# Prompt attention: a unit's last key block is transposed ahead of its first one, and each of the two waits for the query tiles that it reads alone

## The reference

```python
k = mla_keys(c_kv, k_r, w_uk, ...)                     # (T, 8 heads, 96)
v = jnp.einsum('btr,rhv->bthv', c_kv, w_uv)            # (T, 8 heads, 128)
s = jnp.einsum('bqhd,bkhd->bhqk', qi, k) * SCALE
s = jnp.where(k_pos[None, :] <= q_pos[:, None], s, -jnp.inf)
p = jax.nn.softmax(s, axis=-1)
o = jnp.einsum('bhqk,bkhv->bqhv', p, v)
```

## Time and profile before

| | us |
|---|---|
| median of 3 runs | 2067.64 (2067.43 to 2069.14) |
| the profiled execution, and its span | 2069.43, 2067.6 |
| PE busy | 2027.0 (98% of the span) |
| DVE busy | 1273.2 (62%) |
| ACT busy | 857.2 (41%) |
| POOL busy | 551.9 (27%) |
| mean granted TensorE clock | 0.997 of full |

### The profile page before, as it was taken

The page is one execution under the profiler, slowest core; times in us unless marked ns, Lnnn a source line. Parts: engine busy times, 40 slices in busy tenths (PEclk is TensorE's granted clock), DMA queues, the critical chain, the costliest instruction groups (busy, mean ns, idle before and its releaser), DMA issues.

```text
span 2067.6 us, 35685 instructions
## 1 busy us (share of the span) xinstructions
PE 2027.0 (98%) x12489; PEld 1866.4 (90%) x12489; DVE 1273.2 (62%) x2492; ACT 857.2 (41%) x1691; POOL 551.9 (27%) x562
## 2 busy tenths in 40 slices
PE   7999999999999999999999999989999999999999
PEld 6889999988889999999999978879988899998888
DVE  5674411277777777767767753576666656666665
ACT  5552111166656656666665642422222222222221
POOL 2210000044431334534553520022232222223220
PEclk9999999999999999999999999999999999999999
DMA  5243222335322222222222161101211111121112
GB/s 173 83 107 80 63 85 84 100 98 153 108 72 78 73 72 68 63 67 69 67 62 71 55 237 43 42 21 47 76 41 41 41 41 41 43 79 41 41 41 87
DMA packets 146270, 152.41 MB, mean 74 GB/s; under 512 B 50710, under 2 KB 122118, under 8 KB 145101
## 3 DMA queue, kind: packets, MB, share of 16 engines
q1 hardware_dynamic: 140405, 128.02, 20.6%
q0 software_dynamic: 5728, 22.65, 3.4%
HBM read 124.77 MB, written 25.97 MB: 73 GB/s over the span
## 4 chain that ended last, share of the span: by engine, by line
PE 88%; DVE 5%; ACT 3%; issue 2%; DMA 1%; SPq 0%; POOL 0%; ACTq 0%; DVEq 0%
PE ps L105 16%; PE ps L2324 16%; PE ps L107 16%; PE ps L106 16%; PE ps L859 12%; PE ps L1755 2%; PE ps L819 2%; PE ps L1472 1%; PE ps L1714 1%; PE ps L1720 1%; PE ps L2413 1%; DVE pa_ntop L1319 1%; PE ps L776 1%; PE ps L869 1%; ACT pa_prob L1234 1%
## 5 line engine op out<-in xcount | busy, mean ns | idle before, releaser
L2576 DVE TENSOR_TENSOR t_m<-t_m,ps 128x512 f32<-128x512 f32 x256 | 172.1, 685 | 112.6 <-PE ps L107 112.6
L1828 ACT ACTIVATE sq<-ps 128x512 f32<-128x512 f32 x256 | 153.3, 599 | 204.0 <-PE ps L107 202.8
L105 PE MATMUL ps<-f_late_h 128*128 128x512 f32 x512 | 200.2, 391 | 7.4 <-issue 6.9
L106 PE MATMUL ps<-f_late_l,f_late_h 128*128 128x512 f32 x512 | 200.0, 391 | 0.0
L107 PE MATMUL ps<-f_late_h,f_late_l 128*128 128x512 f32 x512 | 199.8, 390 | 0.0
L1915 DVE TENSOR_REDUCE ss<-sq 128x8 f32<-128x512 f32 x256 | 173.0, 676 | 0.0
L2429 POOL TENSOR_TENSOR f_bl<-f_x,f_bh 128x512 fp32r<-128x512 f32 x45 | 59.6, 1325 | 364.5 <-ACT f_bh L2419 364.5
L1913 DVE TENSOR_TENSOR g_attn_b<-ps,g_attn_b 128x64 f32<-128x64 f32 x256 | 56.8, 222 | 147.1 <-ACT sq L1828 145.5
L105 PEld LDWEIGHTS ps<-f_late_h 128*128 128x128 f32 x512 | 96.5, 188 | 27.8 <-issue 8.1
L2519 ACT ACTIVATE f_late_h<-f_raw 128x2048 fp32r<-128x2048 f32 x15 | 28.8, 1919 | 219.9 <-PE ps L107 219.9
L107 PEld LDWEIGHTS ps<-f_late_h,f_late_l 128*128 128x128 f32 x512 | 96.5, 189 | 20.2
(11 more groups left out here) (473 smaller groups left out, 6313.1 us busy)
## 6 DMA issues: line engine op xcount, KB each, us to landing
f_raw<-in_w_ff SPq DMA_DIRECT2D x32, 1024.0 KB, 5.8
c_ring<-in_cache_kv_latent SPq DMA_DIRECT2D x192, 128.0 KB, 2.0
m_raw<-in_w_in SPq DMA_DIRECT2D x20, 512.0 KB, 4.0
gated<-gate POOLq DMA_DIRECT2D x8, 1088.0 KB, 4.8
pa_gm<-gated SPq DMA_DIRECT2D x16, 512.0 KB, 4.6
c_early<-in_cache_kv_latent SPq DMA_DIRECT2D x64, 128.0 KB, 2.0
fr_x<-in_x_prompt SPq DMA_DIRECT2D x8, 512.0 KB, 3.7
mixed<-pa_mixed SPq DMA_DIRECT2D x16, 256.0 KB, 2.1
```

What stands on the lines that cost most here:

```text
L105: nc.tensor.matmul(out, lh, rh, start=first, stop=False)
L106: nc.tensor.matmul(out, lh, rl, start=False, stop=False)
L1828: nc.scalar.activation(sq[:, j % 2, :].rearrange("p (a n) -> p a n", a=2), ps[:, kn_bank(j):kn_bank(j) + 2, 0:HALF], ACT.Square).then_inc( ...
L2576: nc.vector.tensor_tensor(out, out, ps[:, 4 + p % 4, :], ALU.add).then_inc(S["y"], 1)
```

## The change

`order_of` puts the last block ahead of block 0: 4, 0, 1, 3, 2 and 8, 0, 1, 7, 2, 6, 3, 5, 4. Everything else in the list of items stays, the banks too. The wait for the scaled row tiles now stands at both of the first two blocks, each for the tiles that it reads alone: the narrow block for the first scaled tile of the unit, block 0 for all four. Block 0 must still be the first product of the unit, so the narrow block's product is now issued behind it. In units with pieces between the blocks, block 0's product thereby moves from item 5 to item 6, behind that item's piece. The slot wait of a unit's fifth block counts one product more.

```diff
     def order_of(qc):
         rest = [kt for kt in range(NK) if P * kt - META < QC * (qc + 1)]
-        head = [rest.pop(0)]
+        head = [rest.pop(-1), rest.pop(0)]
         while rest:
-            head.append(rest.pop(-1))
+            head.append(rest.pop(0))
             if rest:
-                head.append(rest.pop(0))
+                head.append(rest.pop(-1))
         return head
...
+    first_blocks = [block_no[blocks_of[u][0]] for u in range(len(units))]
...
                     if block_no[n] >= 4:
-                        act.wait_ge(S["pv"], block_no[n] - 3)
+                        act.wait_ge(S["pv"], block_no[n] - 3 + (block_no[n] - 4 in first_blocks))
...
-                if j == blocks_of[u][0] and u:
+                if kt == 0 and u:
                     pe.wait_ge(S["out"], u)
...
-            firsts = [blocks_of[u][0] for u in range(len(units))]
+            firsts, seconds = ([blocks_of[u][k] for u in range(len(units))] for k in range(2))
...
                         if n == blocks_of[p][0]:
                             if p == 0:
                                 pe.wait_ge(S["padded"], SEQ // P - 1)
-                            pe.wait_ge(S["scaled"], NT * (p + 1))
+                        if n in blocks_of[p][0:2]:
+
+                            pe.wait_ge(S["scaled"], NT * (p + 1) - max(0, i - 1 - NT * qc))
...
-                if n - 4 in firsts:
-                    product(n - 4)
                 if n - 3 in block_no and n - 3 not in firsts:
                     product(n - 3)
+                if n - 3 in seconds:
+                    product(firsts[seconds.index(n - 3)])
```

## The result

| | before | after |
|---|---|---|
| median of 5 runs (us) | 2069.14 (2067.43 to 2071.79) | 2079.03 (2076.87 to 2079.93) |
| the profiled execution, span | 2069.43, 2067.6 | 2079.13, 2077.4 |
| PE busy | 2027.0 | 2030.1 |
| mean granted TensorE clock | 0.997 | 0.996 |

The change makes the kernel slower: 1.0046 times before [1.0035, 1.0057], 9.9 us by these medians. The median of before is that of the three runs known ahead (2067.64) and two more. The instruction counts of PE, DVE, ACT and POOL are the same. PE is busy 3.1 us longer with the same matmuls, a first sign that some of them ran at a lower clock; the rest of the difference is time in which PE stands idle.

The account below looks back on a forecast made before the run. PE was taken to bound the prompt's attention (busy 547.21 of 550.00 us). Losses of 0.3 + 1.1 + 2.85 + 0.65 + 2.6 = 7.5 us on 2069.43, less 1.79, gave 2075.1 us; 8-in-10 range 2067 to 2079.5.

Parts of the forecast that it names:

- the clock's case: Units 4 and 8: PE stands still 2.9 us and the clock falls, 3.4 us more, 2078.5; chance 0.10.
- Part 1: First block of units 3, 7, 11, 13: work moved ahead of the wait for POOL gains 1.5 us, at most 3.5.
- Part 2: Units 2, 6, 10: item 6's projection waits for the wide low half behind the gate; 1.0 us late.
- Part 3: Units 3, 7, 11: exponential ahead of the wide copy delays the gate; 0.95 us per pair with the unit before, 0.65 for 12, 13.
- Part 4: Units 4 and 8: low half 0.53 us later and the covering product now behind the projection; 1.3 us each, 2.6 together.
- Part 5: Units 1, 5, 9: PE's fifth item waits for the now wide low half behind the gate; 0.37 us net each, 1.1 together.
- Part 6: The rest: unit 0 loses 0.3 us; units 14 and 15 and the stricter slot wait cost nothing.
- the small gain: Rival: waits at POOL shrink and nothing else moves; 1.5 us won, 2066.1; chance 0.15.
- the faster one: Rival: gate follows the narrow low half at once in units 1, 5, 9, 4, 8; 4.15 us won, 2063.5; chance 0.07.
- The clock's rival: Units 4 and 8: the long stand-still of PE lowers the clock, 1.7 us each, 2078.5; chance 0.10.

Follow-up runs that it names:

- e6: The changed kernel with POOL subtracting only 16 of 1024 columns of q's low half for heads 2 to 7; 2071.51 us, 1.001 times before.
- e4: The changed kernel with DVE's low half put between the gate's multiplication and addition; 2069.07 us, 0.9999 times before.
- e8: The changed kernel with item 1's exponential behind item 2's copy in units 3, 7, 11, 13, DVE's reciprocal one item later; 2080.37 us, 1.0043 times before.
- e3: The changed kernel with eight unread matmuls more on PE ahead of item 6's projection in units 4 and 8; 2077.46 us, 1.0038 times before.
- e2: The change made in odd units alone, even units keeping the order of before; 2072.91 us, 1.0013 times before.
- e7: The kernel before with the stricter slot wait alone; 2069.81 us, 1.0002 times before.
- e9: The kernel before with DVE's low half between the gate's steps and, in even units 2 to 12, the addition four items later; 2066.4 us, 0.9982 times before.
- e10: The changed kernel with DVE's low half between the gate's steps and, in even units 2 to 12, the addition four items later; 2068.13 us, 0.9992 times before.
- e5: The kernel before with DVE's low half put between the gate's multiplication and addition; 2067.2 us, 0.9988 times before.
- e1: The change made in even units alone, odd units keeping the order of before; 2077.2 us, 1.0036 times before.

## Why the prediction was right, and where it was not

The direction was right and the size short: a sum of 7.5 us, against 9.4 by units and 9.9 by the medians. The forecast, 2075.1, is 3.9 us under the median: 2.4 of these are the size, 1.5 the base, since it started from 2067.64 and before's median with two more runs is 2069.14. The measured 2079.03 lies within the range by 0.5 us, and just above the forecast's own range (2071 to 2079): it is covered because the range was drawn out to the clock's case, which had a chance of 0.10.

- **Part 1** (four waits for POOL won in part): the waits went. But "L1475's wait for POOL is still there in units 3, 7, 11, about as long" was wrong, and by the prediction's own numbers: PE comes 1.0 late and does 0.37 more ahead of the wait, the scaling is about 0.6 late, so 0.82 becomes 0.05. The timeline of unit 3 shows none, and one of 0.5 is left in the prompt's attention. Since the times followed from the sum and not from that sentence, they held.
- **Part 2** (1.0 for each of units 2, 6, 10): measured 0.97, 0.96, 0.96, by the step foreseen; e6 shows the cause in POOL's subtraction and e4 in DVE's order. The wait itself is 0.67 where I wrote about 0.9: the view counts it from the transposes' end (458.05), whereas the product that stood there in the kernel before started 0.24 ahead of theirs (457.31 and 457.55).
- **Part 3** (0.95 for each pair, 0.65 for 12 and 13): 0.93, 0.92, 0.89 and 0.53. e8 shows the reversed order of copy and exponential, with 0.3 for each odd unit.
- **Part 4** (**1.3 us** each for units 4 and 8): 2.59 and 2.48. **This is the term that was mis-sized.** The low half and the product behind the projection cost 1.02 and 1.06 (e3), a little under 1.3: in e3's unit 4 the scores of item 7 are 1.17 later than in before, counted from the unit's first scores, and 0.16 come back behind them. The other 1.57 and 1.42 are the clock. I had it as a rival with a chance of 0.10, priced at 1.7 each, and argued from waits of 1.0 us at the same place that left the clock alone. They say nothing on one of 2.79: the prediction itself had worked out 2.9 us in one piece. The rule that it named, of the Trainium skill, TensorE: Matmul & The Clock Gate, section "Why this matters for your kernels", is that gaps between bursts of matmuls drop the clock, and the trace agrees: it fell in both units. The page says only roughly how long a gap must be, and 2.79 us stands at the edge of its wording, so it did not settle the case ahead of the run. In e6's profile 1.63 us in the same place did not lower the clock.
- **Part 5** (0.37 for each of units 1, 5, 9): 0.35, 0.33, 0.35. In e2, with even units as before, they pay the same: the order of the odd unit alone does it.
- **Part 6**: unit 0 lost nothing where 0.3 was forecast, units 14 and 15 nothing beyond the queries' stretch, the slot wait nothing (e7).

Parts 2 and 3 come to 3.3 us, part 4 to 5.1, part 5 to 1.0, u15 to 0.2. Waits were forecast at some 16 us, the view has 14.4. Of the rivals, the small gain did not come, and the faster one failed on both its conditions. The gate did not follow the narrow low half at once, and it was not POOL that stood between, as the prediction had it: in unit 4 DVE first waits 2.38 us for ACT's copy of the values (`pa_v`, 481.44), 2.37 before, and less the 1.4 that the units ahead hand over the multiplication starts when it did before (482.79 and 481.36). And PE did wait for the wide low half behind the gate. The clock's rival, 2078.5, is 0.5 us under the median, in part by luck: its sum of 10.9 is 1.0 too large and its base 1.5 too low.

What stays open: e4 leaves 0.16 to 0.48 in units 3, 7, 11 and 13, and wins 0.39 in units 1, 5 and 9; I have no experiment that takes these apart.

## What to carry to other kernels

When two blocks are swapped to shorten one wait, look where their follow-up work lands in the other engines' queues: here most of the loss came from a 0.69 us instruction that fell behind one that took 1.85 beside another engine's instruction, and putting the instruction that frees a bank ahead of the one that frees nothing brought the time back to that of before. Forecast not only the sum of PE's waits but how long it stands still in one piece: here the long pause cost the wait and then the slower matmuls behind it, and the second part was the larger one (1.57 and 1.42 us against 1.02 and 1.06). And try such a repair on the old kernel too: with the two moves on DVE the kernel before (e9) is ahead of the changed one (e10). To put the held instruction one place later only moved the wait (e5); to put it behind the subtractions left 0.3 us of it (e9).

## What the runs showed of the hardware that I had not expected

In ten of the twelve profiles the clock stands low for a while at the samples' queries (612.7 in the earlier trace rows), though PE is busy, and the length differs from profile to profile: none in e1 and e7, 3.4 us in after, some 6.8 in e2 and e3. e7, e2 and after:

```profile
606.00:616.00 10.00, 10.00 (x86) 9.26 (x85) 7.17 (x15) 4.98 (x13) 3.12 (x4) 1.00 0.25 79
```

```profile
613.80:620.60 6.80, 6.80 (x40) 6.45 (x39) 2.40 (x5) 1.12 (x3) 0.96 (x2) 0.50 0.15 58
```

```profile
622.70:626.10 3.40, 3.40 (x22) 3.17 (x21) 1.45 (x3) 0.43 (x3) 0.00 (x0) 0.50 0.00 0
```

Measured against before this is worth from -1.5 (e1) to +2.0 us (e9) in u15. It may be much of the spread between runs of one kernel, which one profile for each cannot show; effects of 1 to 2 us were therefore read by units and not from the median. The low stretch behind the stand-still in units 4 and 8 was there in all three kernels profiled with it (after, e1, e8), 3.4 us long, but once, in e8, 10.2, although PE was busy for 9.09 of them.
